# Low key parts on all 128 rows, page numbers kept for the value loads, and the last row's thirds added ahead of the reciprocals

## The reference

```python
# layer 0, sparse attention: 8 query heads, 2 kv heads of width 64
s = einsum('btkgd,bnkd->bkgtn', qg, k) * (B_HD ** -0.5) - slopes * dist   # three branches
p = masked_softmax(s, mask)                                               # compressed, selected, window
o = g[..., 0:1] * o_cmp + g[..., 1:2] * o_slc + g[..., 2:3] * o_win
# samples: selected pages of keys and values by page_table
phys = page_table[bi, jp // bpp];  r_past = pool_r[phys, sub, :, li_idx, :, gi, :]
# behind each mixer and each feed-forward part
x = x + y;  h = x * rsqrt(mean(x * x, -1) + EPS) * w
```

## Time and profile before

| | us |
|---|---|
| median of three runs | 3011.74 |
| the three runs | 3006.05, 3011.74, 3014.43 |
| the profiled execution | 3007.39 |
| its span, first to last instruction | 3005.1 |
| PE busy in the span | 2817.0 (94%) |
| DVE busy | 1263.2 (42%) |
| ACT busy | 1152.3 (38%) |
| POOL busy | 400.3 (13%) |
| mean granted TensorE clock, share of full | 0.968 |

### The profile page before, as it was taken

How to read it: one execution, slowest core, us unless ns; L and a number is a source line. 1 busy time by engine, 2 the same in 40 slices (tenths; PEclk the granted TensorE clock), 3 DMA queues, 4 the chain that set the end, 5 groups by cost and what they waited for, 6 DMA issues and landing times.

```text
span 3005.1 us, 47516 instructions
## 1 busy us (share of the span) xinstructions
PE 2817.0 (94%) x18103; PEld 1841.7 (61%) x18103; DVE 1263.2 (42%) x2043; ACT 1152.3 (38%) x1593; POOL 400.3 (13%) x578
## 2 busy tenths in 40 slices
PE   4889988996999999899999999899998999999997
PEld 2667666654555556566666666566664666666664
DVE  7245555232444454644444321532336444443223
ACT  4665755221555552444444211311114444443111
POOL 2312302322000000211111000111102111111000
PEclk9899989997999999999999999999999999999999
DMA  3322223462000021111111111111111111111111
GB/s 112 88 73 64 73 60 112 124 192 74 1 1 1 1 85 43 42 49 49 49 49 52 62 56 46 34 49 54 50 51 36 49 49 49 49 53 64 48 49 66
DMA packets 113484, 173.20 MB, mean 58 GB/s; under 512 B 16993, under 2 KB 83922, under 8 KB 112978
## 3 DMA queue, kind: packets, MB, share of 16 engines
q1 hardware_dynamic: 92610, 150.90, 15.6%
q0 software_dynamic: 3792, 12.58, 1.3%
q10 hardware_dynamic: 16960, 8.16, 0.9%
HBM read 161.47 MB, written 14.30 MB: 58 GB/s over the span
## 4 chain that ended last, share of the span: by engine, by line
PE 81%; DVE 7%; SPq 5%; ACT 4%; issue 2%; DMA 1%; DVEq 0%; ACTq 0%
PE PS L1729 64%; PE PS L2053 5%; PE PS L2067 2%; PE PS L2024 2%; PE PS L2025 2%; DVE R L1191 2%; ACT xT L827 2%; PE PS L1762 2%; PE PS L1709 2%; SPq L456 1%; SPq L461 1%; SPq L532 1%; SPq L529 1%; DVE R L1185 1%; PE PS L1830 1%
## 5 line engine op out<-in xcount | busy, mean ns | idle before, releaser
L1729 PE MATMUL PS<-hT,R 128*128 128x344 f16 x10152 | 1495.5, 310 | 20.3 <-ACT R L840 14.7
L1729 PEld LDWEIGHTS PS<-hT,R 128*128 128x128 f16 x10152 | 996.4, 98 | 516.9 <-ACT R L840 15.2
L506 DVE SCALAR_TENSOR_TENSOR R<-W,R 128x1024 f16<-128x1024 f32 (+1 forms) x186 | 247.7, 1333 | 985.4 <-ACT R L500 984.9
L500 ACT ACTIVATE R<-W 128x1024 f16<-128x1024 f32 (+1 forms) x186 | 206.4, 1110 | 924.4 <-PE PS L1729 918.5
L1729 PE MATMUL PS<-R 128*128 128x344 f16 x3276 | 478.2, 309 | 0.0
L1729 PEld LDWEIGHTS PS<-R 128*128 128x128 f16 x3276 | 320.6, 98 | 157.2
L672 POOL TENSOR_TENSOR hT<-R,hT 128x344 f16<-128x344 f32 x48 | 48.2, 1005 | 848.6 <-ACT hT L773 848.6
L1625 DVE SCALAR_TENSOR_TENSOR R<-R 128x1024 f32<-128x1024 f32 x96 | 123.2, 1284 | 79.5 <-ACT R L1134 78.3
L2053 PE MATMUL PS<-R 128*64 128x256 f32 (+1 forms) x592 | 154.9, 391 | 1.1 <-ACT R L1031 0.9
L1031 ACT ACTIVATE R<-PS 128x512 f32<-128x512 f32 (+1 forms) x160 | 85.8, 565 | 136.6 <-PE PS L2067 136.2
L827 ACT ACTIVATE xT<-xT 64x1024 f32<-64x1024 f32 x64 | 124.6, 1947 | 23.4 <-DMA xT<-cmp_t 22.0
(11 more groups left out here) (293 smaller groups left out, 2596.7 us busy)
## 6 DMA issues: line engine op xcount, KB each, us to landing
W<-wk SPq DMA_DIRECT2D x154, 512.0 KB, 3.4
W<-wdn SPq DMA_DIRECT2D x32, 704.0 KB, 4.1
xT<-cmp_t SPq DMA_DIRECT2D x256, 64.0 KB, 1.9
xT<-x SPq DMA_DIRECT2D x16, 516.0 KB, 6.8
o_y<-hT SPq DMA_DIRECT2D x6, 688.0 KB, 3.5
o_win_s<-state_win POOLq DMA_DIRECT2D x1, 4088.0 KB, 23.9
R<-s_hgrn POOLq DMA_DIRECT2D x4, 512.0 KB, 5.3
o_hgrn_s<-R ACTq DMA_DIRECT2D x4, 512.0 KB, 3.2
```

The source lines that it names most:

```text
L500: act.activation(to[:, n, 0, 0:width], W[:, n, 0:width], ACT.Copy, scale=UNIT).then_inc(wh_here, 1)
L506: dve.scalar_tensor_tensor(to[:, n, 1, 0:width], W[:, n, 0:width], UNIT, to[:, n, 0, 0:width], ALU.mult, ALU.subtract).then_inc(w_split, 1)
L1729: ins = pe.matmul(wide(u)[:, m, :], weights[half], src[:, other, m * TW:(m + 1) * TW], start=(first and half == other == 0), stop=(last an ...
```

## The change

The low key parts are written for both halves of the partitions, in another place and at twice the size, and the second matmul of a pair takes all 128 rows. Page numbers loaded for a sample's keys are kept in registers and used again for its values where the same engine issues both (samples 4 and 6 on SP, 7 on POOL, 5 on ACT). SP's load of the distance table moves ahead of values 4 and 6, and PE takes the samples in the order 0, 1, 2, 3, 5, 7, 4, 6. In the tails of the two stages the second third is added and summed ahead of the first reciprocal, ScalarE's second root moves behind four high parts, and the mean of the first third stands one feature block later in PE's stream.

```diff
-        KY = halves(xf[:, 6208:7232]).rearrange("p (c n) -> p c n", c=2)
+        KY = halves(reg(8256, 2048)).rearrange("p (c g n) -> p c g n", c=2, g=2)
...
-        def pages_of(engine, first, what, dst, signal, free):
+        def pages_of(engine, first, what, dst, signal, free, held=None):
+            numbers = list(held or [])
             for half in range(0, NPG, 8):
-                pages = [engine.value_load(pg[0:1, first + half + n:first + half + n + 1], min_val=0, max_val=NPOOL - 1)
-                         for n in range(8)]
+                if not held:
+                    numbers += [engine.value_load(pg[0:1, first + half + n:first + half + n + 1], min_val=0, max_val=NPOOL - 1)
+                                for n in range(8)]
                 if half == 0:
                     free()
...
-            for b in (4, 6):
-                key_pages(sp, b)
-            for b in (0, 2, 4, 6):
+            held = {b: key_pages(sp, b) for b in (4, 6)}
+            for b in (0, 2):
                 value_pages(sp, b)
             wait_full(sp, U_S + 6)
             sp.dma_start(TAB, table).then_inc(tab_in, 16)
+            for b in (4, 6):
+                value_pages(sp, b, held[b])
...
-            key_pages(pool, 7)
-            for b in (3, 7):
-                value_pages(pool, b)
+            held = key_pages(pool, 7)
+            value_pages(pool, 3)
+            value_pages(pool, 7, held)
...
                 root_third(norm, 0)
                 square_third(norm, 1, v)
+                high_third(norm, 0, range(0, 2))
+                square_third(norm, 2, v)
+                high_third(norm, 0, range(2, 4))
                 root_third(norm, 1)
-                high_third(norm, 0, range(0, 4))
-                square_third(norm, 2, v)
...
-                for c in range(2):
-                    dve.tensor_tensor(KY[rows, c, :], KVT[rows, 2 + c, 0:T], KX[rows, c, half, :], ALU.subtract
+                for to in (rows, slice(64 - 64 * half, 128 - 64 * half)):
+                    for c in range(2):
+                        dve.tensor_tensor(KY[to, c, half, :], KVT[rows, 2 + c, 0:T], KX[rows, c, half, :], ALU.subtract
...
                 sum_third(norm, 0)
-                one_over(norm, 0)
                 add_third_of(norm, 1, v)
                 sum_third(norm, 1)
-                rows_third(norm, 0, range(0, 4))
+                one_over(norm, 0)
+                rows_third(norm, 0, range(0, 2))
                 add_third_of(norm, 2, v)
-                rows_third(norm, 0, range(4, 6))
+                rows_third(norm, 0, range(2, 4))
                 sum_third(norm, 2)
-                rows_third(norm, 0, range(6, KD))
+                rows_third(norm, 0, range(4, KD))
...
-            for b in range(NB):
+            for turn, b in enumerate((0, 1, 2, 3, 5, 7, 4, 6)):
...
-                    return pe.matmul(out, q[rows], low, start=False, stop=True)
+                    return pe.matmul(out, q, low, start=False, stop=True)
...
-                            if (m, f) in ((1, 5), (2, 7)):
+                            if (m, f) in ((1, 6), (2, 7)):
                                 mean_third(after, m - 1)
```

More of the change, by code:

```diff
@@ L245, in program @@
         KX = halves(xf[:, 4160:6208]).rearrange("p (c g n) -> p c g n", c=2, g=2)
-        KY = halves(xf[:, 6208:7232]).rearrange("p (c n) -> p c n", c=2)
-        CX, CY = halves(xf[:, 4096:4160]).rearrange("p (g n) -> p g n", g=2), halves(reg(28608, 32))
+        KY = halves(reg(8256, 2048)).rearrange("p (c g n) -> p c g n", c=2, g=2)
+        CX, CY = (halves(v).rearrange("p (g n) -> p g n", g=2) for v in (xf[:, 4096:4160], reg(28608, 64)))
         QS = halves(hf[:, 4128:8224]).rearrange("p (h n) -> p h n", h=HB)
@@ L451, in spans @@
                     (0, slice(T + 640, T + 640 + NCP)))
-        def pages_of(engine, first, what, dst, signal, free):
+        def pages_of(engine, first, what, dst, signal, free, held=None):
+            numbers = list(held or [])
             for half in range(0, NPG, 8):
-                pages = [engine.value_load(pg[0:1, first + half + n:first + half + n + 1], min_val=0, max_val=NPOOL - 1)
-                         for n in range(8)]
+                if not held:
+                    numbers += [engine.value_load(pg[0:1, first + half + n:first + half + n + 1], min_val=0, max_val=NPOOL - 1)
+                                for n in range(8)]
                 if half == 0:
                     free()
-                for n in range(8):
-                    engine.dma_start(dst(half + n), what[ds(pages[n], 1)].rearrange("a p b -> p a b")).then_inc(signal, 16)
+                for n in range(half, half + 8):
+                    engine.dma_start(dst(n), what[ds(numbers[n], 1)].rearrange("a p b -> p a b")).then_inc(signal, 16)
+            return numbers
         def key_pages(engine, b):
@@ L469, in free, with value_pages @@
                     engine.wait_ge(key_used, b - 4)
-            pages_of(engine, b * NPG, slc_kt, lambda j: KEYS[b % 5].unsqueeze(1)[:, :, j * P:(j + 1) * P], key_in[b], free)
-        def value_pages(engine, b):
+            return pages_of(engine, b * NPG, slc_kt, lambda j: KEYS[b % 5].unsqueeze(1)[:, :, j * P:(j + 1) * P], key_in[b], free)
+        def value_pages(engine, b, held=None):
             def free():
@@ L485, in free @@
                     wait_full(engine, U_S + 5)
-            pages_of(engine, b * NPG, slc_v, lambda j: VALUES[b][:, j:j + 1, :], value_in[b], free)
+            pages_of(engine, b * NPG, slc_v, lambda j: VALUES[b][:, j:j + 1, :], value_in[b], free, held)
         STEP, at_step = {}, 0
@@ L986, in _ @@
             exponentials(1, PC[:, 0:NCS], 0)
-            key_pages(act, 5)
+            held = key_pages(act, 5)
             exponentials(2, SW, 2)
@@ L990, in _ @@
             exponentials(3, SX, 1)
-            value_pages(act, 5)
+            value_pages(act, 5, held)
             wait_full(act, U_S + 6)
@@ L1424, in _ @@
                 rows = slice(64 * half, 64 * half + 64)
-                for c in range(2):
-                    dve.tensor_tensor(KY[rows, c, :], KVT[rows, 2 + c, 0:T], KX[rows, c, half, :], ALU.subtract
+                for to in (rows, slice(64 - 64 * half, 128 - 64 * half)):
+                    for c in range(2):
+                        dve.tensor_tensor(KY[to, c, half, :], KVT[rows, 2 + c, 0:T], KX[rows, c, half, :], ALU.subtract
+                                          ).then_inc(kl_here, 1)
+                    dve.tensor_tensor(CY[to, half, 0:NCP], KCP[rows, 0:NCP], CX[rows, half, 0:NCP], ALU.subtract
                                       ).then_inc(kl_here, 1)
-                dve.tensor_tensor(CY[rows, 0:NCP], KCP[rows, 0:NCP], CX[rows, half, 0:NCP], ALU.subtract).then_inc(kl_here, 1)
             wait_full(dve, U_S + 4)
@@ L1998, in _ @@
                                     stop=(t == NPG - 1), skip_group_check=True)
-                if b % 4 == 3:
+                if turn % 4 == 3:
                     ins.then_inc(o8_full, 1)
@@ L2017, in first @@
                 if n < 2:
-                    pe.wait_ge(kl_here, 6)
+                    pe.wait_ge(kl_here, 12)
                 if i == NC - 1:
@@ L2032, in first @@
                         keys = slice(key, key + end - lo)
-                        scores(psf[:, lo:end], KX[:, c, half, keys], KY[rows, c, keys])
+                        scores(psf[:, lo:end], KX[:, c, half, keys], KY[:, c, half, keys])
                         lo, key = end, key + end - lo
-                scores(psf[:, cmp], CX[:, half, 0:NCP], CY[rows, 0:NCP]).then_inc(sc_full, 1)
+                scores(psf[:, cmp], CX[:, half, 0:NCP], CY[:, half, 0:NCP]).then_inc(sc_full, 1)
             def second(m):
```

## The result

| | before | after |
|---|---|---|
| median, us | 3012.59 (3006.05 to 3014.43, 4 runs) | 2930.74 (2926.60 to 2934.90, 4 runs) |
| profiled execution, us | 3007.39 | 2929.75 |
| its span, us | 3005.1 | 2927.7 |
| first score of the prompt at | 736.42 | 718.50 |
| from there to the first product of mix_out | 371.88 | 315.67 |

The ratio is 0.9732, with a 95% interval from 0.9712 to 0.9753. The kernel is 82 us faster. Both large terms can be read off two starts in TensorE's timeline: the first score comes 17.9 us earlier, and the prompt's attention is 56.2 us shorter.

A forecast was written before the change was run, and what follows sets the result against it. PE, busy 94% of the span, was taken to bound the kernel, with SP's loads holding the samples' values. 3007.4 - 55 - 18.9 - 1.4 = 2932.1 us, forecast as 2934 for a median; 8-in-10 range 2922 to 2953.

The forecast's parts named there:

- A: Prompt's attention: VectorE takes over, 12.6 us of the saving from i = 3 lost, values 6 late by 5: 2950 us; chance 0.11.
- B: Scores: the 0.1 us is not the shape's, pairs keep 0.64, 0.32 and 0.27 us: 2991 us; chance 0.05.
- Scores: Prompt's attention on PE: shape change removed twice in each of 280 pairs, 0.21 us less a pair; sum 55 us.
- the 4.4 us: Scores: sum smaller by this if 176 matmuls of 128 columns save 0.025 us less each, by a page's 81 ns.
- the upper bound: Scores: 59 us, the full 0.21 us for all 280 pairs and nothing lost.
- the 1.3 us given back: Scores at i = 0: subtracted because ScalarE's copies and exponentials fill nearly the whole turn while a unit's scores shrink 0.6 us.
- A step's price: PE's change of shape: 0.15 us for the step to the 64-column product, some 0.1 us in each matmul of a pair.
- Low key parts: VectorE's doubled subtractions, about 5.1 us more: cost nothing under the cover of SP's loads, 2.7 us without it.
- Page numbers: Samples' values: kept page numbers let SP issue values 4 and 6 sooner; 18.9 us, between 17.7 and 20.2.
- the forecast's two prices: Sample 2 on PE: 3.66 us at the higher clock or 6.17 as now; the middle, 4.9, was taken.
- Tails: Tails of mix_out and conv_out: second reciprocal about 0.7 us earlier; 1.4 us for two, bounds +1 and -3.
- C: Prompt's attention: clock goes to 1.2 GHz from i = 3 on, kernel slower: 3034 us; chance 0.03.

The follow-up runs named there:

- 64 rows behind: Changed kernel with the low pass of the scores on 64 rows, in each unit all low products behind all high ones: 2941.39 us.
- other weights: Changed kernel with the low pass taking the queries of the head before, for three heads of four, still on 128 rows: 2931.20 us.
- 64 rows in turn: Changed kernel with the low pass of the scores on 64 rows again, high and low products alternating, key parts still written twice: 2990.75 us.
- the second profile: Changed kernel run once more without any edit, to stand beside runs of the same chip: 2930.83 us.

## Why the prediction was right

**The sum.** The profiled execution was forecast at 2932.1 us and took 2929.75. The three terms together came out within 0.1 us of their forecast (56.2 + 17.9 + 1.3 against 55 + 18.9 + 1.4); the other 2 us lie behind the prompt's attention, where two executions of one kernel differ by 4.6. The 2934 us for a median don't follow from the working: 2932.1 with the 4.35 us added that it names are 2936.5, and no row gives another term. Measured were 2930.74, 1.0 above the profiled execution. The chances of the forecast, A and B add up to 0.97, where the working has 0.96. Neither slip changes the range.

**Scores: 55 us forecast, 56.2 measured.** The mechanism and the paces were right: 0.44, 0.11 and 0.06 us a pair, where 0.43, 0.11 and 0.06 were worked out from streams of one shape. A product of 128 columns takes 0.056 us, so the 4.4 us that the forecast set beside its sum were not lost. The runs with 64 rows behind, with other weights and with 64 rows in turn leave no other cause. Two small terms were mis-sized and nearly cancel. The second half of the pairs with 63 columns was thought lost to the turn's weight load; the turn starts 0.03 us behind the last product, so all 0.21 us are saved, 64 x 0.04 = 2.6 us more, and the sum becomes the upper bound, 58.9. And PE's waits for VectorE's copies out of the banks grew by more than the 1.3 us given back. Waits of PE (engine and line, releaser: us in total, times, longest) in the first units and behind them, of the kernel before and then of the kernel after:

```profile
PE PS L2024 <- DVE R L1486: 6.8, 3, 2.3
...
PE PS L2024 <- DVE R L1486: 4.4, 13, 0.5
```

```profile
PE PS L2031 <- DVE R L1493: 7.9, 3, 3.4
...
PE PS L2031 <- DVE R L1493: 5.8, 13, 0.6
```

They grew by 1.1 and 1.4 us, 2.5 in all: 58.9 - 2.5 = 56.4. The forecast found the single waits unchanged, apart from i = 0. That step was mis-sized: the short waits stand in every block from i = 3 on, and nearly each is 0.12 us longer (0.64 where it was 0.53 at i = 3). The 1.1 us of the first units are one wait, ahead of the fourth. VectorE's timeline shows the scaling of the first unit (`weighted`), in the kernel before and then in the kernel after:

```profile
748.89 1.38 DVE L1509 TENSOR_SCALAR R<-R 128x1024 f32<-128x1024 f32 x3
```

```profile
727.77 3.99 DVE L1516 TENSOR_SCALAR R<-R 128x1024 f32<-128x1024 f32 x3
```

The same three operations take 2.6 us longer and hold up the copy for which PE waits. GpSimd works beside them until 731.25 in the kernel after, and was done at 748.83 in the kernel before; that this is the reason wasn't tested. In both profiles of the kernel after the fourth unit starts 15.35 us behind the first score, though PE's products of the third were done earlier in the second profile, where the clock stayed at 1.00 for 12 us behind the first score (in the first profile it was 0.54 from 4 to 8 us behind it) and the three waits come to 10.5 us. There rival A is true: VectorE sets the pace.

**A step's price, as the forecast had it.** It took 0.15 us from four turns with the step behind them, and 0.1 us a product from the pairs. Both held: 0.29 us for the two steps of a group with value products, 0.1 for a pair's. The page "TensorEngine Tiling (Array Packing)" of the Trainium skill (Key Properties) says that a change of tiling mode drains TensorE. That would fit the runs, with 0.1 to 0.2 us for a step; that the steps are such changes of mode, no run here shows.

**Low key parts: nothing, forecast and measured.** PE starts its turns at 674.56 where 674.8 was worked out, and the run with six subtractions shows the cover: it was the wait for sample 2's pages behind SP's loads, as named.

**Page numbers: 18.9 us forecast, 17.9 measured.** Values 4 and 6 are issued from 689.66 to 705.06 (688.6 to 705.3 forecast), the table held nothing up, and PE runs five samples at 4.12 us each without a gap. The term that was off is sample 2: it starts at 690.86, not 690.27, and takes 5.33 us, not 4.9; together 1.0 us. That it came so close is in part luck. In the second profile of the kernel after, the first score is 21.2 us ahead of the kernel before's: sample 2 took 3.66 us there, the lower of the forecast's two prices, and SP's values 0 and all behind them came some 1.7 us sooner. The run that loads the numbers again takes 16.5 us more, which shows the mechanism.

**Tails: 1.4 us forecast, 1.3 measured** (2 x 0.64), by the way that was given: the first reciprocal and rows come a little later (7.30 us behind the first add against 7.00), and the 0.92 us wait for the high part is gone. PE's stretches above show both tails 0.64 us shorter.

**The rivals.** A (VectorE takes over) was right in its direction and in one place, the fourth unit: 2.5 us instead of 12.6. B fell with the run on 64 rows. C (the clock falls from i = 3 on) didn't come: 1.00 from 893 to 1025, with PE busy for 126.09 of 132.00 us. But the same thing happened on a small scale where the forecast didn't look, in the first units: with 64 rows and the earlier start, the lower level lasted through 745, and the first five units took 5.2 us longer than in the kernel before. The kernel after gained 4.0 us there.

## What to carry to other kernels

Read starts, not lengths, and look for products that alternate in how many rows or columns of the array they use: a step between 128 and 64 or 63 rows, or between 128 and 64 columns, cost 0.1 to 0.2 us here, and filling the array with copies or zeros removed it (56 us for the scores, 19 for the values, 10 for 63 rows). Where the same numbers are needed twice, keep them in registers if SP's queue is on the chain; and before you cost work on another engine, add up the waits behind it, for what it delays may be covered by the next one.

## What was not expected of the hardware

A product on 64 rows costs nothing by itself, and the runs show nothing else for 63. In the run with wide value products the group of two products on 128 rows and two on 63 takes 1.23 us, and on 128 rows alone 0.95. Read from the starts of single products, the 0.28 us are three parts of about 0.1: the last product on 128 rows takes 0.309 us, the first on 63 takes 0.320, the last on 63 takes 0.309, where 0.216 is the pace without a step. It looks as if products on 63 rows were slow. But where a value product on 128 rows follows one on 63, it takes 0.320 us as well, all eight times in that run (at 980.06 for one), and the one behind it is back at 0.216 wherever PE has no wait. So the price is the step's, on both sides of it. Whether 64 rows in place of 63 would change it for this product was not tried.

A doubled output costs nothing: value products on 128 columns of the array with 256 columns to stream keep 0.22 us each (0.87 / 4, in the run with wide values), and the 64-column ones between themselves take 0.216.
